# Moving dense products between the small products of the delta-rule (RWKV-7) branch

## The chip, the cores and the metric

The kernel runs on one core of one Trainium2 chip. The metric is the device time of one launch in microseconds (us). TensorE (PE in the profile) multiplies, VectorE (DVE) and ScalarE (ACT) do the elementwise work, SyncE (SP) issues the transfers. Each has its own instruction stream, and they meet only at semaphores.

## The reference, cut to what matters

Two layers of a decoder step on 256 prompt tokens and 8 sequences of 4 sample tokens, so 288 token columns. Each layer runs three recurrent branches (retention, GLA, RWKV-7), gates each of them with a sigmoid of a projection, adds them, and ends in a feed-forward part. The part that matters is the RWKV-7 branch and the gated output products of the other two branches, which the kernel computes inside it:

```python
def step(S, xs):                                   # rwkv7_scan, per token
    r_t, w_t, k_t, v_t, kk_t, a_t = xs
    sa = jnp.einsum('bhvk,bhk->bhv', S, -kk_t)
    S = (S * w_t[:, :, None, :] + sa[..., None] * (kk_t * a_t)[:, :, None, :]
         + v_t[..., None] * k_t[:, :, None, :])
    y = jnp.einsum('bhvk,bhk->bhv', S, r_t)
    return S, y
...
gates = jax.nn.sigmoid(p_merge).reshape(B, T, N_BRANCH, D_MODEL)
merged = (gates[:, :, 0] * (y_ret @ wb[0]) + gates[:, :, 1] * (y_gla @ wb[1])
          + gates[:, :, 2] * (y_rw @ wb[2]))
```

## The kernel before, in words

`rwkv` runs once a layer and loops in Python over eight head pairs (`for i in range(KT)`, KT = 8), each pair on the 128 partitions, 64 a head. The tokens are cut into chunks of 64: four of the prompt and one that holds the samples. In a chunk the recurrence becomes a triangular system whose inverse is built by doubling, in five levels n = 0 to 4. A level is two groups of small products with a copy between them:

- `level_w(i, n)` (L1001): 64x64 products of AT and X into bank W. ScalarE's `take_w(i, n)` copies them to W1.
- `level_x(i, n)` (L1009, and L1014 in levels 0 to 3) multiplies W1 into bank XX. VectorE's `level(i, n)` (L1411 to L1414) puts the masked result into X and XT, on which the next `level_w` waits.

Between these stand other small groups, `to_tokens` (L994: transposes of v, b, k and at), and products of the full array: `variance(i - 1)` (L1147, not in pair 0), `key_norm(i + 1)` (L956) and, partly in a layout of 64 rows by 128 columns, `lora_up(i + 1)` (L949 to L951). The last two are not in pair 7. A matmul in fp32 stands in the trace as two instructions, called passes below; in the listings of the order it is one.

To fill TensorE while the other engines copy, `Between` deals out *dense products*, 128x128 by 128x288, one matmul each (L272), whenever `side(n)` is called with n. They are a list of four slabs of eight products for each pair: slabs 0 and 1 project hT to the two gates, into banks 6 and 7; slab 2 multiplies y_ret into bank 6 again, and slab 3 y_gla into bank 7. Pair i's loop body deals the 32 products of pair i + 1, so pair 7 has none left. Before a slab's first product stands a wait:

```python
def side_wait(i, j):
    if j < 2 and i >= 1:
        pe.wait_ge(sig("side_used"), 2 * i - 1 + j)
    elif j >= 2:
        pe.wait_ge(sig("gates"), i + 1)
    slab_arrived(pe, S_SIDE, i, j)
```

The signal "gates" comes from ScalarE's `gates(i)`: it waits until slab 1 is done, takes both sigmoids out of banks 6 and 7, signals, and loads the table for `key_scale(i)`, which follows it. In ScalarE's stream of pair i the order is `take_w(i, 3)`, `gates(i + 1)`, `key_scale(i + 1)`, `take_w(i, 4)`, `decays(i + 1)`. The stream of each engine is written out by hand; nothing reorders it.

Of the kernel before, what the change touches and what calls it, by code (L numbers as in the profile page):

```python
# [190 lines left out]
def build(nc, xT_in, w_mix, w_lora, w_rank, w_gkup, vec_in, vecf_in, router_in, w_ff, s_ret, s_gla, s_rw,  # L191
# [185 lines left out]
    def heads_of(ap, hh):  # L377
        return ap[64 * hh:64 * hh + 64]
# [476 lines left out]
    def rwkv(nc, block, sig, layer):  # L855
# [33 lines left out]
        def unit(ap, c):  # L889
            return ap[:, CH * c:CH * c + CH]  # L890
# [37 lines left out]
        def _(pe):  # L928
            mm = nc.tensor.matmul
# [8 lines that stand above are left out]
            side = Between([(lambda i=i, j=j: side_wait(i, j), j, SIDE_BANK[j % 2][:, 0:T], (hT, hT, y_ret, y_gla)[j])  # L938
                            for i in range(KT) for j in range(4)])

            def lora_up(i):
                pe.wait_ge(sig(f"wr{i % 2}"), i // 2 * 16 + 16)
                if i == 0:
                    pe.wait_ge(sig("th"), 1)
                else:
                    pe.wait_ge(sig("vtok"), i)
                    pe.wait_ge(sig("btok"), i)
                    pe.wait_ge(sig("ktok"), i)
                mm(LORA_W[:, 0:T], wr[0:64, i % 2, 0:128], th[0:64, :], start=True, stop=True)  # L949
                mm(LORA_A[:, 0:T], wr[64:128, i % 2, 0:128], th[64:128, :], start=True, stop=True)  # L950
                mm(LORA_G[:, 0:T], wr[:, i % 2, 128:256], sg, start=True, stop=True).then_inc(sig("up"), 1)  # L951

            def key_norm(i):
                pe.wait_ge(sig("kk2"), i + 1)
                pe.wait_ge(sig("sw"), i + 1)
                mm(P1[:, 0:T], headones, kk2, start=True, stop=True).then_inc(sig("kk_ps"), 1)  # L956

            def bonus_sum(i):
                pe.wait_ge(sig("rk"), i + 1)
                mm(P2[:, 0:T], headones, rk, start=True, stop=True).then_inc(sig("rk_ps"), 1)  # L960
# [30 lines left out]
            def to_tokens(i, out, src, n, name):  # L991
                for c in range(n):
                    for h in range(2):
                        last = mm(unit(heads_of(out, h), c), src(h, c), heads_of(eye64, h), start=True, stop=True)  # L994
                last.then_inc(sig(name), 1)

            def level_w(i, n):
                pe.wait_ge(sig("X"), i * (nlev + 1) + n + 1)
                for c in range(5 if n == 0 else 4):
                    for h in range(2):  # L1000
                        last = mm(unit(heads_of(W, h), c), heads_of(AT, h)[:, c], heads_of(X, h)[:, c],  # L1001
                                  start=True, stop=True)
                last.then_inc(sig("W1_ps"), 1)

            def level_x(i, n):
                pe.wait_ge(sig("W1"), i * nlev + n + 1)
                for c in range(4):
                    for h in range(2):
                        last = mm(unit(heads_of(XX, h), 4 + c), heads_of(W1, h)[:, c], heads_of(XT, h)[:, c],  # L1009
                                  start=True, stop=True)  # L1010
                if n < nlev - 1:
                    for c in range(4):
                        for h in range(2):
                            last = mm(unit(heads_of(XX, h), c), heads_of(XT, h)[:, c], heads_of(W1, h)[:, c],  # L1014
                                      start=True, stop=True)
                if n == 0:
                    for h in range(2):
                        last = mm(unit(heads_of(W, h), 5), heads_of(W1, h)[:, 4], heads_of(XT, h)[:, 4],
                                  start=True, stop=True)
                last.then_inc(sig("X_ps"), 1)  # L1020

            def right_side(i):
                pe.wait_ge(sig("X"), i * (nlev + 1) + nlev + 1)
                pe.wait_ge(sig("vtok"), i + 1)
                for c in range(4):
                    for h in range(2):
                        mm(unit(heads_of(W, h), c), heads_of(PkPr, h)[:, c, 0], heads_of(vtok, h)[:, c],
                           start=True, stop=True)
                pe.wait_ge(sig("aseq"), i + 1)
                for h in range(2):  # L1030
                    mm(unit(heads_of(W, h), 4), heads_of(Ps, h)[:, 1], heads_of(vtok, h)[:, 4], start=True, stop=False)
                for b in range(NB):
                    for h in range(2):
                        last = mm(unit(heads_of(W, h), 4), heads_of(aseq, h)[:, b, :],
                                  heads_of(s0m, h)[:, b, :], start=False, stop=(b == NB - 1))
                last.then_inc(sig("R_ps"), 1)

            def key_value(i):
                pe.wait_ge(sig("attok"), i + 1)
                pe.wait_ge(sig("ktok"), i + 1)  # L1040
                for c in range(4):
                    for h in range(2):
                        mm(unit(heads_of(E, h), 3 + c), heads_of(ktok, h)[:, c], heads_of(vtok, h)[:, c],
                           start=(c == 0), stop=False)
# [95 lines left out]
            def mean(i):  # L1140
                pe.wait_ge(sig("o"), i + 1)
                pe.wait_ge(sig("stn"), i + 1)
                mm(E[:, 0:T], headmean, o, start=True, stop=True).then_inc(sig("mean_ps"), 1)

            def variance(i):
                pe.wait_ge(sig("osq"), i + 1)
                mm(E[:, 0:T], headmean, osq, start=True, stop=True).then_inc(sig("var_ps"), 1)  # L1147
# [8 lines left out]
            for i in range(KT):  # L1156
                more = i + 1 < KT
                level_w(i, 0)
                side(3)
                pe.wait_ge(sig("Ps"), i + 1)  # L1160
                if i:
                    mean(i - 1)
                to_tokens(i, P1, lambda h, c: heads_of(proj_pad, h)[:, 2 * KT + i, CH * c:CH * c + CH], 5, "v_ps")
                level_x(i, 0)
                side(1)
                pe.wait_ge(sig("hat"), i + 1)
                to_tokens(i, P2, lambda h, c: unit(heads_of(bh, h), c), 5, "b_ps")
                level_w(i, 1)
                if i:
                    variance(i - 1)  # L1170
                side(2)
                to_tokens(i, P3, lambda h, c: unit(heads_of(kh, h), c), 5, "k_ps")
                level_x(i, 1)
                side(2)
                if i:
                    pe.wait_ge(sig("lnv"), i)
                to_tokens(i, E, lambda h, c: unit(heads_of(ar[i % 2], h)[:, 0], c), 4, "at_ps")
                level_w(i, 2)
                side(2)
                if more:  # L1180
                    lora_up(i + 1)
                level_x(i, 2)
                side(3)
                level_w(i, 3)
                side(3)
                level_x(i, 3)
                if more:
                    key_norm(i + 1)
                side(2)
                level_w(i, 4)  # L1190
                side(3)
                level_x(i, 4)
                key_value(i)
                side(2)
                if more:
                    bonus_sum(i + 1)
                right_side(i)
                side(3)
                solve(i)
                side(1)  # L1200
                carry(i)
                output_early(i)
                chain(i, 1)
                side(1)
                chain(i, 2)
                side(1)
                chain(i, 3)
                side(1)
                solution(i)
                output_state(i)  # L1210
                side(1)
                output_late(i)
                if more:
                    scores(i + 1)
                sample_state(i)
                side(1)
# [1072 lines left out]
```

## Time and profile before

| | |
|---|---|
| median of 3 runs | 3090.67 us (3089.09 to 3090.97) |
| profiled execution: its time | 3093.3 us |
| profiled execution: its span | 3091.5 us |
| TensorE busy | 2896.2 us, 94% of the span |
| weight loads busy | 2374.7 us, 77% |
| VectorE busy | 859.9 us, 28% |
| ScalarE busy | 589.9 us, 19% |

"Busy" of TensorE includes the pipelined tail of each matmul, so in the timeline the time from the start of one group to the start of the next is the better measure. In the first layer pair 0's body runs from 508.6 to 553.2 us of the span, pairs 1 to 6 up to 826.6 us, and pair 7 to some 868 us.

### The profile page before, as it was taken

To read this page: it belongs to the slowest core of one execution; us is meant where nothing else is said; L and a number is where in the kernel's file an instruction comes from. 1 tells how busy PE (TensorE), PEld (TensorE's weight loads), DVE (VectorE), ACT (ScalarE), POOL (GpSimd) and SP (SyncE) were. 2 spreads that over 40 slices of the span, in tenths; PEclk is the share of its full clock that TensorE was granted. 3 is DMA by queue.
4 is the path that set the end of the run, shared out by engine and by line. 5 is a ranking of instruction groups with operands and counts; after the bars stand their busy time and mean duration, and the time that the engine had idled before them with its cause. 6 is when DMAs were issued, how large, how long until landed. Compare 5 with 4: busy or idle time off the path is not lost. (4 is left out here: it accounts for less than half of the span.)

```text
span 3091.5 us, 82764 instructions
## 1 busy us (share of the span) xinstructions
PE 2896.2 (94%) x36666; PEld 2374.7 (77%) x36666; DVE 859.9 (28%) x2370; ACT 589.9 (19%) x1736; POOL 0.2 (0%) x4
## 2 busy tenths in 40 slices
PE   8999998999999999999898999989799999999998
PEld 6776675777777776777676777767688989998987
DVE  2023544555411001112454455441301110111011
ACT  2132322223201000122322233220100110111011
POOL 0000000000000000000000000000000000000000
PEclk9999889999999999999988999999899999999999
DMA  5232313122233334333322222123399889988985
GB/s 209 83 140 89 137 71 101 61 64 62 76 94 129 136 130 146 103 110 110 117 87 113 71 62 68 57 68 123 117 332 340 320 309 346 345 328 314 353 304 208
DMA packets 144521, 497.09 MB, mean 161 GB/s; under 512 B 18608, under 2 KB 23344, under 8 KB 141776
## 3 DMA queue, kind: packets, MB, share of 16 engines
q1 hardware_dynamic: 144208, 492.33, 45.0%
q8 instruction: 268, 4.39, 0.6%
q14 instruction: 45, 0.37, 0.0%
HBM read 471.97 MB, written 20.29 MB: 159 GB/s over the span
## 5 line engine op out<-in xcount | busy, mean ns | idle before, releaser
L349 PE MATMUL bank<-work,ring 128*64 128x96 f32 x16896 | 727.8, 247 | 32.3 <-issue 30.6
L349 PEld LDWEIGHTS bank<-work,ring 128*64 128x64 f32 x16896 | 706.1, 137 | 60.2 <-issue 46.7
L272 PE MATMUL bank<-hT,ring 128*128 128x288 f32 x2048 | 589.7, 433 | 0.4 <-DMA ring<-w_mix_dram 0.4
L272 PEld LDWEIGHTS bank<-hT,ring 128*128 128x128 f32 x2048 | 392.1, 200 | 108.0 <-issue 1.4
L341 PE MATMUL bank<-hT,ring 128*128 128x288 f32 x1024 | 256.9, 412 | 7.7 <-PEq L174 7.7
L341 PEld LDWEIGHTS bank<-hT,ring 128*128 128x128 f32 x1024 | 197.4, 193 | 64.9 <-issue 9.7
L1225 ACT ACTIVATE work<-bank 128x256 f32<-128x256 f32 (+3 forms) x272 | 104.4, 396 | 506.7 <-PE bank L1123 120.7
L1596 PE MATMUL bank<-hT,ring 128*128 128x288 f32 x704 | 172.6, 409 | 1.7 <-DVE hT L1670 1.7
L2145 DVE TENSOR_TENSOR work<-bank,work 128x96 f32<-128x96 f32 x176 | 45.3, 257 | 438.9 <-PE bank L349 438.8
L1596 PEld LDWEIGHTS bank<-hT,ring 128*128 128x128 f32 x704 | 134.7, 191 | 39.6 <-issue 2.1
L2098 ACT ACTIVATE work<-bank 128x96 f32<-128x96 f32 x176 | 44.2, 251 | 451.9 <-PE bank L349 451.9
L2149 DVE TENSOR_TENSOR xT<-xT,bank 128x288 f32<-128x288 f32 x64 | 29.1, 454 | 312.2 <-PE bank L2070 312.2
L272 PE MATMUL bank<-y_gla,ring 128*128 128x288 f32 x256 | 87.2, 440 | 0.0
L341 PE MATMUL bank<-work,ring 128*128 128x288 f32 x352 | 85.5, 406 | 0.0
L341 PEld LDWEIGHTS bank<-work,ring 128*128 128x128 f32 x352 | 66.9, 190 | 18.5
L272 PE MATMUL bank<-y_ret,ring 128*128 128x288 f32 x256 | 76.1, 424 | 0.6 <-ACT work L1225 0.6
L356 ACT ACTIVATE work<-bank 128x256 f32<-128x256 f32 x52 | 20.1, 386 | 254.2 <-PE bank L272 239.9
L1001 PEld LDWEIGHTS bank<-work 64*64 64x64 f32 x1344 | 46.7, 137 | 26.7 <-issue 16.2
L341 PE MATMUL bank<-proj,ring 128*128 128x288 f32 x256 | 64.7, 406 | 0.0
L1001 PE MATMUL bank<-work 64*64 64x64 f32 x1344 | 56.3, 225 | 8.9 <-DVE work L1414 6.7
L2102 ACT ACTIVATE work<-bank 128x96 f32<-128x96 f32 x64 | 16.1, 251 | 254.1 <-PE bank L349 254.1
L1582 PE MATMUL bank<-merged,ring 128*128 128x288 f32 x256 | 62.4, 406 | 0.0
(398 smaller groups left out, 3178.2 us busy)
## 6 DMA issues: line engine op xcount, KB each, us to landing
ring<-w_ff_dram SPq DMA_DIRECT2D x540, 512.0 KB, 5.4
ring<-w_mix_dram SPq DMA_DIRECT2D x256, 512.0 KB, 4.0
ring<-w_ff_dram SPq DMA_DIRECT2D x72, 384.0 KB, 4.7
work<-s_gla_dram SPq DMA_DIRECT2D x8, 1024.0 KB, 9.5
gla_s_out<-work SPq DMA_DIRECT2D x8, 1024.0 KB, 4.8
work<-s_ret_dram SPq DMA_DIRECT2D x8, 512.0 KB, 5.0
ret_s_out<-work SPq DMA_DIRECT2D x8, 512.0 KB, 3.0
work<-s_rw_dram SPq DMA_DIRECT2D x16, 256.0 KB, 2.6
```

The lines of the kernel that those rows point to most:

```text
L272: mm = nc.tensor.matmul(out, ring[:, s, k, :], rhs[:, k, :], start=(k == 0), stop=(k == KT - 1))
L341: mm = nc.tensor.matmul(out, ring[:, s, k, :], rhs[:, k0 + k, :], start=(k0 + k == 0), stop=(k0 + k == last - 1))
L349: mm = nc.tensor.matmul(out[64 * c:64 * c + 64], ring[:, s, k, 64 * c:64 * c + 64], rhs[:, k0 + k, :], start=(k0 + k == 0), stop=(k0 + k = ...
L356: nc.scalar.activation(row[:, r, 1:1 + NP], ps[:, 0:NP], ACT.Copy)
L1001: last = mm(unit(heads_of(W, h), c), heads_of(AT, h)[:, c], heads_of(X, h)[:, c], start=True, stop=True)
L1225: return nc.scalar.activation(out, in_, func, **kw)
L1582: mm = nc.tensor.matmul(OUT[s % 3][:, 0:T], ring[:, s, k, :], merged[:, k, :], start=(k == 0), stop=(k == KT - 1))
L1596: mm = nc.tensor.matmul(bank[n % 4][:, 0:T], ring[:, n % RING, k, :], hT[:, k, :], start=(k == 0), stop=(k == KT - 1))
L2098: ac(act1[:, f % 2, :], bank[2 * f % 4][:, 0:CAP], ACT.Silu).then_inc(sig("w1_free"), 1)
L2102: ac(oT[:, m % 2, :], DOWN[m % 2][:, 0:CAP], cp).then_inc(sig("oT"), 1)
L2145: tt(hid[:, f, :], bank[(2 * f + 1) % 4][:, 0:CAP], act1[:, f % 2, :], ALU.mult).then_inc(sig("w3_free"), 1)
L2149: tt(xT[:, m, :], xT[:, m, :], ADD[:, 0:T], ALU.add).then_inc(sig("added"), 1)
```

## The change

Only numbers of `side(n)` change, in the loop body of TensorE's stream. The call after `variance` and the call after `level_w(i, 2)` go; their four products are dealt in three later calls, and the two of the first in the call after `level_x(i, 1)`. Of a pair's 32 products 11 stand in these calls before (2, 2, 2, 3, 2) and after (4, 4, 3). No product, copy or wait is added or removed.

```diff
                 level_w(i, 1)
                 if i:
                     variance(i - 1)
-                side(2)
                 to_tokens(i, P3, lambda h, c: unit(heads_of(kh, h), c), 5, "k_ps")
                 level_x(i, 1)
-                side(2)
+                side(4)
                 if i:
                     pe.wait_ge(sig("lnv"), i)
                 to_tokens(i, E, lambda h, c: unit(heads_of(ar[i % 2], h)[:, 0], c), 4, "at_ps")
                 level_w(i, 2)
-                side(2)
                 if more:
                     lora_up(i + 1)
                 level_x(i, 2)
-                side(3)
+                side(4)
                 level_w(i, 3)
                 side(3)
                 level_x(i, 3)
                 if more:
                     key_norm(i + 1)
-                side(2)
+                side(3)
                 level_w(i, 4)
                 side(3)
                 level_x(i, 4)
```

On TensorE, in pair 1's body, the first place runs from `variance` (L1147) to `lora_up` (L949); L272 is a dense product, L994 `to_tokens`. Before:

```order
L1147 MATMUL bank<-work,table 128x288
L272 MATMUL bank<-hT,ring 128x288 x2
L994 MATMUL bank<-table,work 64x64 x10
L1009 MATMUL bank<-work 64x64 x8
L1014 MATMUL bank<-work 64x64 x8
L272 MATMUL bank<-hT,ring 128x288 x2
L994 MATMUL bank<-table,work 64x64 x8
L1001 MATMUL bank<-work 64x64 x8
L272 MATMUL bank<-hT,ring 128x288 x2
L949 MATMUL bank<-work 128x288
```

The same place after the change:

```order
L1147 MATMUL bank<-work,table 128x288
L994 MATMUL bank<-table,work 64x64 x10
L1009 MATMUL bank<-work 64x64 x8
L1014 MATMUL bank<-work 64x64 x8
L272 MATMUL bank<-hT,ring 128x288 x4
L994 MATMUL bank<-table,work 64x64 x8
L1001 MATMUL bank<-work 64x64 x8
L949 MATMUL bank<-work 128x288
```

The full-array product of `variance` stays between the small groups, and `lora_up` now follows `level_w(1, 2)` directly. The second place is on the same engine, after `level_x(1, 3)`: `key_norm` (L956), then the side products, then `level_w(1, 4)`.

```order
 L1014 MATMUL bank<-work 64x64 x8
 L956 MATMUL bank<-ring,table 128x288
+L272 MATMUL bank<-hT,ring 128x288
 L272 MATMUL bank<-y_ret,ring 128x288 x2
 L1001 MATMUL bank<-work 64x64 x8
```

The last product of slab 1 (reading hT) stood before `level_x(1, 3)`; it now stands directly ahead of the first product of slab 2 (reading y_ret).

## Rows read from the trace of the kernel before

**Rows 1.** The page's first line.

```profile
span 3091.5 us, 82764 instructions
```

**Rows 2.** Windows: an ordinary pair, then pair 7 of layer 0.

```profile
599.50:645.06 45.56, 45.56 (x750) 35.10 (x747) 24.16 (x66) 13.59 (x34) 0.00 (x0) 1.00 0.19 63
...
826.56:868.98 42.42, 29.70 (x617) 25.61 (x617) 16.50 (x42) 7.49 (x19) 0.00 (x0) 0.78 0.21 77
```

**Rows 3.** Windows, TensorE alone: an ordinary pair of layer 1.

```profile
1771.97:1817.53 45.56, 45.56 (x747) 1.00 0.21 63
```

**Rows 4.** Timeline of an ordinary pair's levels, TensorE: start, length, group.

```profile
650.85 0.75 PE L1147 MATMUL bank<-work,table 128*128 128x288 f32 x2
...
652.51 0.80 PE L994 MATMUL bank<-table,work 64*64 64x64 f32 x20
653.14 0.63 PE L1009 MATMUL bank<-work 64*64 64x64 f32 x16
653.61 0.63 PE L1014 MATMUL bank<-work 64*64 64x64 f32 x16
654.17 1.24 PE L272 MATMUL bank<-hT,ring 128*128 128x288 f32 x4
655.34 0.68 PE L994 MATMUL bank<-table,work 64*64 64x64 f32 x16
655.85 0.63 PE L1001 MATMUL bank<-work 64*64 64x64 f32 x16
656.41 1.24 PE L272 MATMUL bank<-hT,ring 128*128 128x288 f32 x4
657.58 0.51 PE L949 MATMUL bank<-work 64*128 64x288 f32 x1
...
658.95 0.68 PE L1009 MATMUL bank<-work 64*64 64x64 f32 x16
...
660.03 1.72 PE L272 MATMUL bank<-hT,ring 128*128 128x288 f32 x6
661.68 0.68 PE L1001 MATMUL bank<-work 64*64 64x64 f32 x16
662.29 1.72 PE L272 MATMUL bank<-hT,ring 128*128 128x288 f32 x6
663.95 0.68 PE L1009 MATMUL bank<-work 64*64 64x64 f32 x16
...
665.02 0.75 PE L956 MATMUL bank<-ring,table 128*128 128x288 f32 x2
665.61 1.13 PE L272 MATMUL bank<-y_ret,ring 128*128 128x288 f32 x4
666.67 0.68 PE L1001 MATMUL bank<-work 64*64 64x64 f32 x16
...
668.94 0.68 PE L1009 MATMUL bank<-work 64*64 64x64 f32 x16
```

**Rows 5.** Timeline of the same stretch, ScalarE; in brackets the idle time and its releaser.

```profile
650.50 0.85 ACT L1225 ACTIVATE work<-bank 128x320 f32<-128x320 f32 x2 [1.69 <-PE bank L994]
...
656.06 0.85 ACT L1225 ACTIVATE work<-bank 128x256 f32<-128x256 f32 x2 [2.28 <-PE bank L994]
...
664.05 0.71 ACT L1225 ACTIVATE work<-bank 128x288 f32<-128x288 f32 x2 [1.26 <-PE bank L272]
...
667.40 0.38 ACT L1225 ACTIVATE work<-bank 128x256 f32<-128x256 f32 x1 [0.35 <-PE bank L1001]
```

**Rows 6.** Timeline of the same stretch, VectorE at level 2.

```profile
660.14 0.45 DVE L1413 COPY_PREDICATED work<-masks,bank 128x256 f32<-128x256 uint8 x1 [1.83 <-PE bank L1014]
```

**Rows 7.** Timeline of pair 7: a copy of ScalarE and the product behind it.

```profile
836.10 0.38 ACT L1225 ACTIVATE work<-bank 128x256 f32<-128x256 f32 x1 [0.70 <-PE bank L1001]
...
836.53 0.68 PE L1009 MATMUL bank<-work 64*64 64x64 f32 x16 [0.48 <-ACT work L1225]
```

**Rows 8.** Timeline of TensorE: the first small group of pair 0.

```profile
508.63 0.80 PE L1001 MATMUL bank<-work 64*64 64x64 f32 x20 [1.09 <-DVE work L1399]
```

## The prediction

> **What bounds the kernel now.** I read the page first. The span is 3091.5 us [rows 1] and TensorE is busy for 94% of it, so the question is what TensorE does in the stretch that the change touches. The windows answer it: in an ordinary pair (1 to 6, both layers) TensorE is busy for all of the 45.56 us [rows 2, 3], with the granted clock at 1.00. There is no wait in such a pair that a later arrival could use up. Whatever TensorE gains or loses in a pair goes straight to the end. Pair 7 is different (29.70 us busy of 42.42 us [rows 2]), but it has no dense products left, so the change leaves its instructions as they were. That leaves seven pairs in each of two layers, 14 in all.
>
> Then I read the timeline of one ordinary pair, measuring from start to start, because the printed lengths overlap.
>
> **What a run of dense products costs.** A run of 4 passes takes 655.34 - 654.17 = 1.17 us until the next small group starts, a run of 6 takes 661.68 - 660.03 = 1.65 us [rows 4]. A pass is therefore 0.24 us, and each run carries 1.17 - 4 x 0.24 = 0.21 us on top, which is paid at its end. Entering a run costs too: a small group of 16 takes 653.61 - 653.14 = 0.47 us before another small group, and 656.41 - 655.85 = 0.56 us before a dense run [rows 4], so 0.09 us. The first small group behind a run takes 0.51 us (655.34 to 655.85) instead of 0.47, another 0.04. A run that vanishes between two small groups thus gives 0.34 us, its passes being paid elsewhere.
>
> The Trainium skill says in "TensorEngine Tiling (Array Packing)", section Key Properties, that a change of tiling mode, though not a change of tile, drains TensorE. The trace agrees in kind (the 0.21 us). Taken by itself that rule speaks for the change: two modes fewer twice a pair would be 0.68 us in each of 14 pairs, 9.5 us faster, an estimate that counts the rows' 0.34 us for each run that the words of the change name.
>
> **The change, run by run, in an ordinary pair.**
>
> 1. After `level_w(i, 1)`. `variance` stays, and it is a full-array product itself. The run from 650.85 to 652.51 (6 passes, 1.66 us) shrinks to 2 passes, 0.69 us, and the run at 654.17 grows from 4 to 8, by 0.96 us. Sum: about 0. No switch is saved.
> 2. After `level_w(i, 2)`. The run of 4 passes (656.41 to 657.58, 1.17 us [rows 4]) goes, and `lora_up` follows the small group. Its 4 passes come back in two later runs that exist already: + 0.96 us. That is -0.21 us. `lora_up` is a 64x128 layout, and no row shows 64x64 going straight into it. If that costs what entering a 128x128 run costs, the 0.09 us stays and the gain is 0.21. If it costs nothing, the gain is 0.30. If it drains like the end of a dense run, the gain is 0. I take 0.21, since the entry into the full array is the nearest row.
> 3. After `key_norm`. Here the order of the slabs meets a wait. Before, the 16th product of the pair, the last of slab 1, ended the run that starts at 662.29. ScalarE's two sigmoids started at 664.05, its idle time before them ended by that product, and ended at 664.05 + 0.71 = 664.76 [rows 5]. The 17th product, which needs "gates", started at 665.61 [rows 4]: 0.85 us of cover, made of `level_x(i, 3)` and `key_norm`. Now the three calls deal 4 and 4 instead of 2, 2, 2 and 3, so only 15 products stand before `level_x(i, 3)`. The 16th comes behind `key_norm`, and the 17th directly behind the 16th. TensorE must wait for both sigmoids with nothing in between.
>
> **The price of that wait.** Let t be the start of `key_norm`. The first dense pass behind it starts at t + 0.59 (665.61 - 665.02), the second pass of the 16th product at t + 0.83. From a last dense pass to the sigmoids: the run at 662.29 has its sixth pass at 662.29 + 5 x 0.24 = 663.49, the sigmoids start at 664.05, so 0.56 us. They start at t + 1.39 and end at t + 2.10. From the end of a ScalarE copy to the product it releases: 836.53 - 836.48 = 0.05 us [rows 7]. So the 17th product starts at t + 2.15. Without the wait it would have started at t + 0.59 + 0.48 = t + 1.07. The wait is 1.08 us. A run that starts anew also pays something that a running one doesn't: the first two passes behind a small group take 0.59 instead of 0.48, so 0.11 more; bounds 0 (the weights may be there already) and 0.2 (the layout's drain in full). I take 0.11.
>
> An ordinary pair changes by -0.21 + 1.08 + 0.11 = **+0.98 us**.
>
> **Pair 0** has no `variance`, so run 1 vanishes whole: -0.34 us more. Then `level_x(0, 1)` comes early for its copy. In the ordinary pair the two copies behind `level_w(i, 1)` start at 650.50 and end at 651.35 [rows 5], and by rows 4 this group starts 0.56 us before 650.85, at 650.29; the copy is ready 1.06 us after it. The product would come after 0.47 + 0.58 = 1.05 us. A wait of up to 0.1 us. I take -0.25 for it.
>
> **Other waits.** `level_x(i, 2)` loses 1.17 us of cover. Before it starts at 658.95, its copy ends at 656.91 [rows 5], 2.04 us earlier; 0.87 are left. The levels' DVE work waits for TensorE (1.83 us idle at level 2 [rows 6]), which now arrives earlier by 1.17 us; 0.66 us are left. Behind `gates` ScalarE has the table load and `key_scale`, then `take_w(i, 4)`: from the start of the sigmoids to the end of `key_scale` is 667.40 - 0.35 - 664.05 = 3.00 us, then 0.38 us for the copy. So W1 is ready at t + 1.39 + 3.00 + 0.4 = t + 4.8. TensorE asks for it at t + 3.92 before (668.94 - 665.02), plus 0.48 for one product more and 1.19 for the wait: t + 5.6. It has 0.8 us of cover only because the first wait already holds TensorE up. VectorE's later steps start from these products. The slab loads behind slab 1 go out a few us later and are needed a whole pair, 45 us, later.
>
> **The sum.** 14 x 0.98 - 2 x 0.25 = +13.2 us. The profiled execution's own time, 3093.3 us, becomes 3106.5; it lies 2.6 us above the median of the runs shown, so against the median of 3090.67 us I expect 3103.9 us. Bounds of the unknowns: the entry into 64x128 (-0.09 to +0.21 a pair, -1.3 to +2.9 us), the new start of the run (-0.11 to +0.09, -1.5 to +1.3 us). The likeliest case's own range is 3101 to 3108 us.
>
> **The rivals.** A measurement of this kernel can tell 0.2%, 6.2 us, from no change.
>
> - *The wait doesn't show* (the case on the other side). The sigmoids would have to be done by t + 1.07, that is 1.08 us sooner than the rows give. Then only the saved runs count: 14 x -0.21 - 0.5 = -3.4 us, 3087.2 us; if the layout change into `lora_up` is free, -4.7 us. For it speaks only that TensorE's ends are modelled; against it the bracket at 664.05, which names the dense product as ScalarE's releaser. It would decide below 0.26 us of wait a pair. With both runs priced at the full 0.34 us the time would be 9.5 us shorter, 3081.2, but `variance` and `lora_up` stand in the places. 5 in 100 for the first, 3 in 100 for the second.
> - *ScalarE's chain holds TensorE a second time.* If the table load is slower to come or `key_scale` gets later than t + 4.4, the 0.8 us of cover before `level_x(i, 4)` is used up. 0.5 us beyond it in each pair is 7 us more, 3111 us. 5 in 100.
> - *The gap costs clock.* In pair 7, with its waits, the clock is 0.78 in the mean [rows 2]. If ordinary pairs fell to that, 45.56 x (1/0.78 - 1) = 12.9 us a pair, 3270 us or more. Against it: at 508.63 TensorE has been idle for 1.09 us, just this length, and the group of 20 behind it takes 0.80 us, as does the group of 20 at 652.51 at full clock [rows 4, 8]. 2 in 100. The Trainium skill, in "TensorE: Matmul & The Clock Gate", section Why this matters for your kernels, warns of idle gaps between bursts because the clock falls back; the row at 508.63 shows no fall after a gap of this length.
> - *Part of the wait is taken up later in the pair.* There is no idle TensorE time in these rows to take it. 3 in 100, some +7 us, 3098.
>
> **How the numbers follow.** My forecast has 82 in 100. The range 3099 to 3109 us holds its own range and an edge for a layout cost at both ends; it leaves out the no-wait case and the clock case. Slower by over 0.2%: 82 + 5 + 2 + 2 = 91 in 100. Within 0.2%: 6. Faster: 3.
>
> **What would show it.** An ordinary pair of 46.5 us in the windows, granted clock 1.00; on TensorE, behind `key_norm`, two dense passes of hT, an idle time of about 1.1 us released by ScalarE (L1225), then four passes of y_ret; the sigmoids 1.4 us behind `key_norm`'s start instead of 1 us before it. `level_w(i, 2)` to `level_x(i, 2)` shorter by 1.17 us, from 3.10 to 1.93. If TensorE doesn't idle at the 17th product, or if a pair is under 45.8 us, the argument is wrong.

## The result, and the profile after

The changed kernel takes 3098.62 us (median of 7 runs, 3087.75 to 3100.65) against 3087.2 us for the kernel before, run beside it (median of 7, three of them those shown above). The ratio is 1.0031, with a 95% interval of 1.0016 to 1.0046: 9.6 us slower, between 4.9 and 14.2. (The two medians themselves lie 11.4 us apart; the ratio is worked out from all the runs.) A second timing of the same two kernels (e1 below) gives 1.0015, 1.000 to 1.003, or 4.6 us. The direction is the forecast one. The forecast was 13.2 us more and a range of 3099 to 3109 us, and the measured median is just below it.

The windows of the changed kernel's profile: an ordinary pair, then pair 7 of layer 0. A row has start and end, length, the busy time and count of PE, PEld (weight loads), DVE, ACT and POOL, then the granted clock as a share of 2.4 GHz, the DMA share and GB/s; a row with one busy time is of PE alone.

```profile
644.14:690.57 46.43, 45.63 (x748) 35.10 (x747) 24.18 (x66) 13.37 (x34) 0.00 (x0) 1.00 0.20 62
829.85:869.27 39.42, 26.58 (x617) 22.82 (x617) 16.52 (x42) 7.49 (x19) 0.00 (x0) 0.89 0.24 83
```

The ordinary pair grew from 45.56 us [rows 2] to 46.43 us, by 0.87 us, and TensorE is now idle for 46.43 - 45.63 = 0.80 us of it. Pair 7, which the change doesn't touch, shrank from 42.42 to 39.42 us, and its mean granted clock rose from 0.78 to 0.89. That was not in the forecast.

The timeline of TensorE in the ordinary pair, from `variance` on, the rows that answer to [rows 4]:

```profile
650.66 0.75 PE L1147 MATMUL bank<-work,table 128*128 128x288 f32 x2
651.34 0.80 PE L994 MATMUL bank<-table,work 64*64 64x64 f32 x20
...
653.00 2.21 PE L272 MATMUL bank<-hT,ring 128*128 128x288 f32 x8
655.14 0.68 PE L994 MATMUL bank<-table,work 64*64 64x64 f32 x16
655.66 0.63 PE L1001 MATMUL bank<-work 64*64 64x64 f32 x16
656.22 0.51 PE L949 MATMUL bank<-work 64*128 64x288 f32 x1
...
657.59 0.68 PE L1009 MATMUL bank<-work 64*64 64x64 f32 x16
...
664.15 0.75 PE L956 MATMUL bank<-ring,table 128*128 128x288 f32 x2
664.74 0.65 PE L272 MATMUL bank<-hT,ring 128*128 128x288 f32 x2
666.19 1.24 PE L272 MATMUL bank<-y_ret,ring 128*128 128x288 f32 x4 [0.80 <-ACT work L1223]
667.35 0.68 PE L1001 MATMUL bank<-work 64*64 64x64 f32 x16
```

and ScalarE beside it:

```profile
665.42 0.71 ACT L1223 ACTIVATE work<-bank 128x288 f32<-128x288 f32 x2 [3.50 <-PE bank L272]
666.15 1.28 ACT L1242 ACT_TABLE_LOAD   x1
667.45 0.50 ACT L1223 ACTIVATE ring<-bank,table 128x288 f32<-128x288 f32 x1
```

Read from `level_w` (655.66) to `level_x` (657.59): 1.93 us instead of 3.10, the run between them is gone. `variance` (650.66) still stands as a full-array product between the small groups. And behind `key_norm` (664.15) the bracket names the wait: the first product of y_ret, at 666.19, was released by ScalarE, whose two sigmoids started at 665.42. They used to start at 664.05, before `key_norm` [rows 5].

### The profile page after: what moved, and what is told of

Its sections match the earlier page's. It is cut to its first block and busy times, and to the rows that moved or that the text cites. A ratio compares the mean times of both kernels' runs of the same rounds, so it can differ in the third digit from the quotient of the medians.

```text
span 3085.9 us, 82764 instructions
## 1 busy us (share of the span) xinstructions
PE 2886.6 (94%) x36666; PEld 2366.4 (77%) x36666; DVE 860.5 (28%) x2370; ACT 587.2 (19%) x1736; POOL 0.2 (0%) x4
## 5 line engine op out<-in xcount | busy, mean ns | idle before, releaser
L272 PE MATMUL bank<-hT,ring 128*128 128x288 f32 x2048 | 587.0, 433 | 0.4 <-DMA ring<-w_mix_dram 0.3
L272 PEld LDWEIGHTS bank<-hT,ring 128*128 128x128 f32 x2048 | 394.4, 201 | 109.2 <-issue 1.4
L272 PE MATMUL bank<-y_ret,ring 128*128 128x288 f32 x256 | 77.6, 430 | 11.8 <-ACT work L1223 11.8
L272 PE MATMUL bank<-y_gla,ring 128*128 128x288 f32 x256 | 87.2, 440 | 0.0
L272 PEld LDWEIGHTS bank<-y_ret,ring 128*128 128x128 f32 x256 | 43.8, 189 | 29.3 <-ACT work L1223 19.1
```

Of the source, the lines that this page charges most:

```text
L272: mm = nc.tensor.matmul(out, ring[:, s, k, :], rhs[:, k, :], start=(k == 0), stop=(k == KT - 1))
```

## The experiments

All pair lengths below are start to start of `level_w(i, 0)` in the profiles. "Pairs 0 to 6" is the time from the start of pair 0 to the start of pair 7, in one layer; it repeats within 0.01 us in all 14 such stretches of the two kernels.

**e1, the changed kernel once more**, beside the next three.

> The changed kernel once more, beside the next three on one chip. Theory (the 17th product waits for the sigmoids): ordinary pairs of 46.43 us, pair 0 of 45.2 us, 0.97 us of idle TensorE before the first product of y_ret; 11.7 us longer than before, ratio 1.0038. Rival (the difference of the first timing came in part from stages that the change doesn't touch): the pairs are the same, but the ratio moves towards 1.000 or beyond 1.005.

3091.54 us against 3086.08 us, ratio 1.0015 (1.000 to 1.003). The pairs are the same as in the first profile (46.43 us, pair 0 45.23 us). So 11.75 us are in the pairs of the two layers, and the whole kernel shows less: the rival holds for a part of the difference.

**e2, 16 products before `level_x(i, 3)`.** Against the changed kernel:

```diff
                 level_x(i, 2)
-                side(4)
+                side(5)
...
                     key_norm(i + 1)
-                side(3)
+                side(2)
```

> The changed kernel with 5 and 2 products instead of 4 and 3 behind level_x(i, 2) and key_norm, so that the 16th product again stands before level_x(i, 3); both removed runs stay removed. Theory: no wait at y_ret, an ordinary pair of 45.56 - 0.21 = 45.35 us, pair 0 0.2 us more off, 3.4 us shorter than before in all, ratio 0.9989. Rival (the removed cover behind level_w(i, 1) and level_w(i, 2) is what costs): the pair stays above 45.56 us and the ratio above 1.001.

Ratio 0.9969 (0.9958 to 0.9980), 9.6 us faster than before. Ordinary pair 45.36 us, pair 0 44.16 us. TensorE's row behind `key_norm`:

```profile
661.51 0.75 PE L956 MATMUL bank<-ring,table 128*128 128x288 f32 x2
662.10 1.13 PE L272 MATMUL bank<-y_ret,ring 128*128 128x288 f32 x4
```

No idle time, 0.59 us behind `key_norm` as before. The removal of the two runs itself gives 0.20 us a pair and 0.43 in pair 0, 3.2 us in all. The kernel gained more than that; see the last section. The rival is refuted: the removed cover costs nothing here.

**e3, the first sigmoid early.** Against the changed kernel, in ScalarE's stream, with TensorE's `side_wait` on `gate{j - 2}`:

```diff
                     sigmoids(i + 1)
+                    gate_out(i + 1, 0)
                 take_w(i, 3)
                 if more:
-                    gates(i + 1)
+                    gate_out(i + 1, 1)
```

> The changed kernel's order on TensorE, but the two sigmoids apart: that of bank 6 stands in ScalarE's stream right behind sigmoids(i + 1), each signals by itself, and the 17th product waits for the first alone. Theory: the wait is gone although the 16th and 17th product still stand side by side; ordinary pair 45.35 us, ratio 0.9989 to before. Rival (a switch of weights or of the bank between slab 1 and slab 2 costs, not the sigmoids): the pair stays at 46.4 us.

Ratio 0.9975 (0.9967 to 0.9984), ordinary pair 45.36 us, and y_ret follows the hT product without a gap. The ratio amounts to 7.7 us, where the pairs give the same 3.2 us as in e2; the 4.5 us beyond them are not explained. The order of TensorE's products is that of the changed kernel, so it is the sigmoids' signal alone that costs, not the change of slab or bank.

**e4, one more run merged.** Against the changed kernel:

```diff
                 level_w(i, 0)
-                side(3)
+                side(4)
...
                 sample_state(i)
-                side(1)
```

> The changed kernel with one more run merged: the last product of a pair, between sample_state(i) and level_w(i + 1, 0), is dealt behind that level_w, in a run of 4 instead of 3. By this 16 products stand before level_x(i, 3). Theory: no wait at y_ret (-1.08 us), and one run fewer between small groups (-0.34 us) against the changed kernel: ordinary pair 45.0 us; 8 us shorter than before, ratio 0.9974. Rival (the last product covers VectorE's start of X, or the product of the means comes too early): TensorE idles before level_w or before mean, pair 45.3 us or more.

Ratio 0.9960 (0.9945 to 0.9975), 12.3 us below the kernel before; ordinary pair 45.02 us, 0.34 us below e2: a run's fixed cost. The pairs give 7.9 of the 12.3 us. It has the lowest ratio of the versions timed more than once, but its interval overlaps that of e2. The rival is right in pair 7 alone: there TensorE is idle for 13.67 us instead of 12.74, as the product of the means now comes too early.

**e5, the wait alone.** Against the kernel before:

```diff
                 level_x(i, 2)
-                side(3)
+                side(2)
...
                     key_norm(i + 1)
-                side(2)
+                side(3)
```

> The kernel before with a single product moved: 2 instead of 3 behind level_x(i, 2), 3 instead of 2 behind key_norm. No run is removed, only the 16th product goes past level_x(i, 3) and key_norm, next to the 17th. Theory: the whole wait without the saved run, 0.97 + 0.11 = 1.08 us a pair, ordinary pair 46.64 us, 15 us longer than before, ratio 1.0049. Rival (cover lost at level_w(i, 2) and level_w(i, 1) has a part in the loss): less than 0.9 us a pair.

Ratio 1.0036 (1.0024 to 1.0048). The ordinary pair takes 46.63 us, 1.07 more than before (1.08 expected), with no run removed: the wait costs this by itself. The whole kernel is 11.1 us slower, not the expected 15. The pairs do give 15.0 us, and pair 7 took 37.99 and 37.98 us, less than in any profile of the kernel before.

```profile
664.80 0.75 PE L956 MATMUL bank<-ring,table 128*128 128x288 f32 x2
...
666.84 1.24 PE L272 MATMUL bank<-y_ret,ring 128*128 128x288 f32 x4 [0.80 <-ACT work L1225]
```

**e6 to e8, the wait by doses**, timed once each. e6 signals each sigmoid by itself:

```diff
                 for n in range(2):
-                    last = ac(gate[:, n, :], SIDE_BANK[n][:, 0:T], ACT.Sigmoid)
-                last.then_inc(sig("gates"), 1)
+                    ac(gate[:, n, :], SIDE_BANK[n][:, 0:T], ACT.Sigmoid).then_inc(sig(f"gate{n}"), 1)
```

> The changed kernel; both sigmoids stay where they are in ScalarE's stream, but each has its own signal, and the 17th product (bank 6) waits for the first one only. Theory: the wait ends one sigmoid earlier, 0.3 to 0.36 us; ordinary pair 46.07 to 46.13 us. Rival (the wait is not that for the sigmoids): 46.43 us.

e7 has a sigmoid more:

```diff
+                ac(spare[:, 0:T], SIDE_BANK[1][:, 0:T], ACT.Sigmoid)
                 last = ac(gate[:, 1, :], SIDE_BANK[1][:, 0:T], ACT.Sigmoid)
```

> The changed kernel with a third sigmoid, of bank 7 into a spare tile, between the two before the signal. Theory: the wait is 0.3 to 0.36 us longer, ordinary pair 46.73 to 46.79 us. Rival: 46.43 us. A second effect, if the forecast of ScalarE's chain holds: level_x(i, 4) still doesn't wait.

e8 puts `key_norm` between the two products:

```diff
+                side(1)
                 if more:
                     key_norm(i + 1)
-                side(3)
+                side(2)
```

> The changed kernel with key_norm between the 16th and the 17th product instead of ahead of both. Theory: its 0.48 us cover half the wait, which falls from 0.97 to 0.49 us; ordinary pair 45.95 us. Rival (another cause): 46.43 us, or more, since key_scale starts later.

Ordinary pairs: 46.13 us (e6), 46.73 us (e7), 45.94 us (e8), each as the theory expected. The rows of y_ret's first product in e6, e7 and e8:

```profile
665.18 1.24 PE L272 MATMUL bank<-y_ret,ring 128*128 128x288 f32 x4 [0.50 <-ACT work L1223]
```

```profile
668.01 1.24 PE L273 MATMUL bank<-y_ret,ring 128*128 128x288 f32 x4 [1.10 <-ACT work L1224]
```

```profile
664.05 1.24 PE L272 MATMUL bank<-y_ret,ring 128*128 128x288 f32 x4 [0.32 <-ACT work L1224]
```

Idle 0.50, 1.10 and 0.32 us against 0.80: a sigmoid less, a sigmoid more, a `key_norm` more of cover (0.48). In e7 `level_x(i, 4)` still starts without a wait. But e8's one time, 3071.75 us, is 20 us below the changed kernel's 3091.54, where its pairs promise 7. Against the profile of e1 it is also shorter by 5.9 us between the two layers' branches and by 9.7 us behind the second. So a single time of this kernel says little of such an edit, and the pair lengths are what to compare.

**e9 to e12, what pair 7 does.** Three more profiles of the kernel before and one of the changed one.

> The kernel before, unchanged, for a second profile. The stretches of the other profiles agree to 0.02 us in pairs 0 to 6, but pair 7, which the change leaves as it was, took 42.42 and 41.96 us before and 39.42 to 40.62 us in the changed kernel, with stretches of half clock that lie differently. Theory (where the half-clock stretches fall is chance from run to run): pair 7 of this kernel varies by 1 us or more between the profiles, and is below 41 us in some. Rival (the length of the pairs ahead, or the order of their products, sets it): 42 us each time.

> The same as the run ahead, a third profile of the kernel before: by the theory pair 7 lies elsewhere between 38 and 42.5 us, by the rival at 42 us.

> A fourth profile of the kernel before, with the same expectations: pair 7 anywhere from 38 to 42.5 us by the theory, at 42 us by the rival.

> A third profile of the changed kernel. Theory: ordinary pairs of 46.43 us again; pair 7 anywhere from 38 to 42.5 us. Rival: pair 7 at 39.4 to 40.6 us as in its first two profiles, so that 3 to 5 us of the 11.7 are given back there.

| kernel | pairs 0 to 6, each layer | pair 7, all stretches profiled |
|---|---|---|
| before (4 profiles) | 317.93 | 42.42, 41.96, 41.97, 41.97, 39.45, 41.95, 42.41, 41.98 |
| changed (3 profiles) | 323.81 | 39.42, 39.43, 40.62, 39.43, 39.47, 39.43 |

Means 41.76 and 39.63 us. Of the six new stretches of the kernel before (e9 to e11) five are at 42 us, as the rival had it, and one at 39.45 us; e12 is at 39.4 to 39.5 us, again as the rival had it. The two kernels overlap in that one stretch, which speaks against chance alone. But the length of the pairs ahead doesn't set it in a simple way either: e6 (pairs 0 to 6 321.69 us) had 39.44 and 41.95 us in its two layers, and e7 (325.93 us) 40.76 and 41.98 us. Pair 7 of the kernel before (e11, both layers) and of the changed one (e12, layer 0), by length, TensorE busy time and granted clock:

```profile
820.77:863.18 42.41, 29.67 (x618) 0.78 0.22 77
2039.63:2081.61 41.98, 29.25 (x618) 0.82 0.22 78
```

```profile
829.98:869.45 39.47, 26.62 (x618) 0.89 0.24 83
```

The work is the same and the busy time isn't: the clock is the difference. Pair 7 has no dense products, TensorE waits 0.4 to 1.6 us at each level, and for a part of it the clock falls to 1.2 GHz, as in the first profile of the kernel before:

```profile
826.56:839.71 13.15, 9.63 (x246) 1.00 0.61 224
839.71:849.95 10.24, 8.25 (x142) 0.50 0.01 2
```

How much of the pair's work that part covers is what varies.

**e13 to e16, the start of pair 7 moved.** In the kernel before, at the end of pair 6, `n` = 2 or 4 products more, whose result is never read:

```diff
                 sample_state(i)
                 side(1)
+                if i == KT - 2:
+                    pe.wait_ge(sig("side_used"), 2 * i + 3)
+                    for _ in range(n):
+                        mm(SIDE_BANK[0][:, 0:T], headones, hT[:, 0, :], start=True, stop=True)
```

> The kernel before with two products more (into a free bank, never read) at the end of pair 6, which put off the start of pair 7 by about 1 us and change nothing else. Theory (the longer pairs shift pair 7 against the stretches of half clock): the first half-clock stretch begins about 1 us earlier seen from pair 7's own start, or one step later, and pair 7 is no longer at 42 us in both layers. Rival (chance alone, or the order of the products in pairs 0 to 6 sets it): with the order of before, pair 7 takes 42 us again, as in 7 of 8 stretches.

> The same kernel once more, since a single profile gives only two lengths of pair 7. Theory and rival as for the run ahead; chance alone would also let the two profiles differ among themselves by 1 us or more.

> As the run ahead with four products more instead of two, so that pair 7 starts about 2 us later than in the kernel before. Theory: pair 7 again moves against the half-clock stretches, to a length other than that with two; rival: 42 us.

> The kernel with four products more once again, for two further lengths of pair 7. Theory: as in its first profile, other than 42 us; rival: 42 us, or any length by chance.

Pairs 0 to 6 grew by 0.97 us (two) and 1.94 us (four), as they should. Pair 7 took 38.64, 40.13, 41.26 and 40.11 us with two, and 39.99, 36.77, 36.77 and 39.99 us with four. None of the eight stretches is at 42. Some 0.57 us of the difference is ordinary cover: the wait before `mean(6)` that pair 7 has otherwise is gone, here in the kernel before:

```profile
827.93 0.75 PE L1143 MATMUL bank<-work,table 128*128 128x288 f32 x2 [0.57 <-DVE work L1405]
```

The rest is clock. The first stretch at 1.2 GHz began 12.9 to 14.0 us into pair 7 in the kernel before, 11.9 to 12.9 us with two products more, which is the theory's "about 1 us earlier", and 14.3 us or only 34.9 us with four. One of the eight stretches, e14's 41.26 us, is little more than the old 42 us without the cover (TensorE busy for 29.08 us against 29.24); the other seven differ by the clock. Where the pair took 36.77 us, it had almost no half clock:

```profile
825.65:862.42 36.77, 24.41 (x617) 0.97 0.23 84
```

In e15, with the same instructions in both layers, the clock alone makes 3.2 us:

```profile
828.74:868.73 39.99, 27.83 (x618) 0.85 0.21 79
2047.14:2083.91 36.77, 24.42 (x618) 0.97 0.23 86
```

So the order of the products in pairs 0 to 6 isn't needed for a shorter pair 7: moving its start by 1 or 2 us was enough in seven of eight stretches. That the 5.87 us longer pairs do the same in the changed kernel fits this and is not shown by itself. Within one kernel pair 7 also differs from profile to profile, by up to 3.2 us.

The whole times say more than that. e13 to e16 took 3077.91, 3078.32, 3076.65 and 3073.21 us, timed once each, against 3087.04 us for the kernel before beside them: 9 to 14 us less, with more work. Against the mean of the four profiles of the kernel before, pair 7 accounts for some 5 us of it. The larger part, some 11 us, is behind the second layer's branch, where TensorE is at work for about as long and idle for less. One of the kernel before (e10) and e16:

```profile
2082.63:3090.35 1007.72, 933.82 (x18468) 0.98 0.79 287
2080.87:3071.37 990.50, 932.45 (x18468) 0.98 0.81 292
```

No run shows what shortens that stretch, or whether the added products have a part in it.

## Why the prediction was right or wrong

**The mechanism was right.** The 17th product waits for the sigmoids at the forecast place (e2, e3 and e5 take the wait away or make it alone; e6 to e8 change it in doses), and `variance` and `lora_up` keep the promised gain small.

**The saved run.** Forecast -0.21 us an ordinary pair; e2 shows 45.36 - 45.56 = -0.20. Entering `lora_up`'s layout costs what I assumed: 656.22 - 655.66 = 0.56 us, as into a full-array run. The Trainium skill's rule that a new tiling mode drains TensorE ("TensorEngine Tiling (Array Packing)", Key Properties) agrees in kind with the fixed 0.34 us of a run that vanishes whole (e4), but it says nothing on which runs vanish.

**The wait.** Forecast 1.08 us. y_ret starts 666.19 - 664.15 = 2.04 us behind `key_norm`'s start, not 2.15, so the wait is 2.04 - 1.07 = 0.97 us. The step that was off is the 0.56 us "from a last dense pass to the sigmoids". It came from placing the sixth pass of the run at 662.29 by five passes of 0.24 us, at 663.49. The trace of the kernel before has it at 663.61, since the first pass of a run takes 0.35 us (the row is of a narrow window that holds this pass alone, as are those of single passes below):

```profile
663.61 0.41 PE L272 MATMUL bank<-hT,ring 128*128 128x288 f32 x1
```

So the sigmoids at 664.05 started 0.44 us behind it. In the changed kernel the second pass of the 16th product and the sigmoids at 665.42 are just as far apart, with nothing on TensorE behind that pass:

```profile
664.98 0.41 PE L272 MATMUL bank<-hT,ring 128*128 128x288 f32 x1
```

And so they are in e8, where `key_norm` follows the pass:

```profile
662.85 0.41 PE L272 MATMUL bank<-hT,ring 128*128 128x288 f32 x1
663.29 0.71 ACT L1224 ACTIVATE work<-bank 128x288 f32<-128x288 f32 x2 [3.02 <-PE bank L272]
```

The 0.11 us was in the prediction already, as the price of a run that starts anew (0.59 instead of 0.48), and was left out where the sixth pass was placed. For the same reason the 0.21 us that a run carries is not all "paid at its end": 0.11 is in its first pass, some 0.10 in its last. The restart itself was sized right: 667.35 - 666.19 = 1.16 us for 4 passes, where a running one takes 1.06 [rows 4]. Sum -0.20 + 0.97 + 0.10 = +0.87 us a pair against +0.98 forecast: 14 x 0.11 = 1.5 us too much.

**Pair 0.** Forecast 0.25 below the others' growth; measured +0.64 against +0.87, so 0.23.

**Pair 7 is the step that failed.** "The change leaves its instructions as they were" is true, and I took its time as unchanged with it: a term put at nothing. It gave back 2 x (41.76 - 39.63) = 4.3 us. With it the stretches from pair 0 to pair 7 give 11.75 - 4.26 = 7.5 us for the whole kernel, which lies between the two timings (9.6 and 4.6 us) and within both intervals. Why pair 7 is shorter in the changed kernel is shown down to the granted clock (0.85 to 0.89, against 0.78 to 0.82 in seven of the eight stretches before), and not further.

**The rest of the kernel** was put at nothing too. Outside pairs 0 to 7 the four profiles of the kernel before took 2363.0 to 2373.1 us and the three of the changed one 2359.5 to 2366.1 us. That spread is larger than what pair 7 gave back, so the 7.5 us are a sum of the parts that repeat, and no proof of the whole.

**The reference time.** I set the sum on the three runs' 3090.67 us; all seven have a median of 3087.2. From the forecast 3103.9 us one takes 3.5 for the reference, 1.5 for the pairs and 4.3 for pair 7, which leaves 3094.7; the measured median is 3098.62. These 3.9 us are open, and it is luck that the forecast missed by only 5.3. The range of 10 us was too narrow for a kernel whose single runs lie 16 us apart (3079.5 to 3095.84 in 28 runs of the kernel before) or 25 (3074.53 to 3099.98 in 11 of the changed one).

**The clock rival** is refuted in its own place: no ordinary pair lost clock by the 0.8 us of idle time (1.00 in the window). The clock moved elsewhere and the other way: pair 7, which does lose clock, lost less of it. The rivals "doesn't show", "a second time" and "taken up later" are each refuted by the pair lengths.

## What to carry to other kernels

When filler work is moved, count through its own list: what matters is not how many pieces stand in a gap but which piece ends up next to which wait. A product that needs another engine's answer to the product just ahead of it wants other work between the two (here 0.8 us), and the best answer was to keep that and merge runs elsewhere. In a kernel with stretches at half clock, an untouched stretch can change its time as well (pair 7 by 2.1 us in the mean); compare stretch by stretch first, and read the whole time only against many runs.

## What the runs showed of the hardware

- A run of full-array products between 64x64 groups costs 0.34 us beyond its passes (0.24 us each at 2.4 GHz); e4 shows the same 0.34 us. Of it 0.11 us is in the first pass, which takes 0.35 us; a run that starts again after the wait pays it too (1.16 us instead of 1.06 for 4 passes).
- From the start of the last dense pass to the ScalarE instruction that waits for it: 0.44 us, whether nothing follows the pass (the changed kernel), a full-array product (e8) or a 64x64 group (the kernel before).
- The same 618 matmul instructions of pair 7 took 36.77 to 42.42 us, the granted clock in the mean being 0.97 to 0.78. With 1 or 2 us of dense products more just ahead of them they took 36.77 to 41.26 us, against 39.45 to 42.42 us without; some 0.57 us of that is a wait that the added products cover.
- Stretches that no edit touched vary too. From the end of layer 0's branch to pair 0 of layer 1 e1 took 858.54 us and e2 852.19 us, in which TensorE was busy for 812.26 and 805.64 us:

```profile
870.45:1728.99 858.54, 812.26 (x3987) 0.95 0.35 117
```

```profile
862.26:1714.45 852.19, 805.64 (x3986) 0.96 0.35 118
```

All seven profiles of the kernel before and the changed one have 858.4 to 858.8 us here, e4 and e8 have 852.7 us like e2, and the granted clock is 0.96 instead of 0.95. e2 gained 9.6 us where its pairs give 3.2; in its profile 3.9 us came from pair 7 (39.81 and 39.79 us) and 6 us from here, more than the difference asks for. What sets where the clock falls in these stretches is left open.
